# Token choice of the expert mixture on eight partition groups an expert, the prompt's residual rows stored after the first gather, and more unread transposes

## What is computed

```python
aff = jax.nn.softmax((xt @ router_w).astype(F32), axis=-1)
gates, idx = lax.top_k(aff.T, cap)          # cap = 2 * n_tok // 16
xe = xt[idx]
hid = jax.nn.silu(einsum(xe, w_gate)) * einsum(xe, w_up)
ye = einsum(hid, w_down) * gates[..., None]
y = zeros.at[idx.reshape(-1)].add(ye.reshape(-1, D))
```

## Time and profile before

| | |
|---|---|
| median of three runs | 2438.5 us |
| slowest and fastest run | 2439.77 and 2438.33 us |
| span of the profiled execution | 2439.0 us (within the range of the runs) |
| PE busy | 2353.6 us, 96% |
| DVE busy | 1783.9 us, 73% |
| ACT busy | 1362.2 us, 56% |
| POOL busy | 299.5 us, 12% |
| DMA | 577.38 MB, mean 237 GB/s |

### The profile page before, as it was taken

How to read it: one execution, slowest core, us unless ns; L and a number is a source line. 1 busy time by engine, 2 the same in 40 slices (tenths; PEclk the granted TensorE clock), 3 DMA queues, 4 the chain that set the end, 5 groups by cost and what they waited for, 6 DMA issues and landing times.

```text
span 2439.0 us, 34267 instructions
## 1 busy us (share of the span) xinstructions
PE 2353.6 (96%) x12062; PEld 1959.1 (80%) x12062; DVE 1783.9 (73%) x2053; ACT 1362.2 (56%) x1494; POOL 299.5 (12%) x360
## 2 busy tenths in 40 slices
PE   8999999999989999999999999998789999999997
PEld 7888888888768888888878888877578888888876
DVE  7565566465878888888865677765578888888854
ACT  5233233233457777777763555443257777777762
POOL 1000000000111112211111100000111211121011
PEclk9999999999989999999999999998899999999999
DMA  6424333223599999999970534231599999999931
GB/s 236 133 80 137 108 109 126 72 90 103 194 374 395 395 390 389 396 391 393 349 193 17 144 100 112 83 99 61 202 339 388 396 394 390 390 391 394 347 125 43
DMA packets 210973, 577.38 MB, mean 237 GB/s; under 512 B 24384, under 2 KB 65856, under 8 KB 210752
## 3 DMA queue, kind: packets, MB, share of 16 engines
q1 hardware_dynamic: 193584, 526.35, 57.7%
q0 software_dynamic: 17296, 49.83, 8.0%
HBM read 547.80 MB, written 30.43 MB: 237 GB/s over the span
## 4 chain that ended last, share of the span: by engine, by line
PE 90%; DVE 4%; DMA 3%; issue 1%; ACT 1%; POOL 0%; SPq 0%; DVEq 0%; POOLq 0%; ACTq 0%
PE bank L1575 43%; PE bank L1459 40%; PE bank L1396 4%; PE bank L1761 1%; PE bank L1743 1%; DMA rows_normed<-xn_late 1%; DVE d_parts L619 1%; DMA m_x<-rows_normed,idx_t 0%; DMA rows_summed<-m_y,idx_out 0%; DMA resid<-in_x_sample 0%; DMA raw<-in_ret_w_in 0%; ACT d_parts L610 0%; DVE top_i L1988 0%; DMA resid<-rows_summed 0%; DVE m_at L1990 0%
## 5 line engine op out<-in xcount | busy, mean ns | idle before, releaser
L2128 DVE TENSOR_TENSOR w_parts<-wt,w_parts 128x2048 fp32r<-128x2048 f32 x384 | 874.6, 2290 | 135.9 <-ACT w_parts L1157 126.1
L1157 ACT CAST w_parts<-wt 128x2048 fp32r<-128x2048 f32 x384 | 734.3, 1913 | 197.2 <-PE bank L1575 186.3
L1575 PE MATMUL bank<-w_parts,m_xt 128*128 128x512 f32 x2976 | 689.5, 391 | 2.1 <-ACT m_y L1215 2.1
L1575 PEld LDWEIGHTS bank<-w_parts,m_xt 128*128 128x128 f32 x2976 | 556.2, 188 | 117.6 <-issue 2.9
L1459 PE MATMUL bank<-d_parts,xt 128*128 128x512 f32 (+1 forms) x1872 | 383.4, 361 | 4.5 <-DVE d_parts L619 4.4
L1575 PE MATMUL bank<-w_parts,m_hidt 128*128 128x512 f32 x1632 | 384.0, 395 | 2.8 <-DVE m_hidt L2120 2.8
L1459 PEld LDWEIGHTS bank<-d_parts,xt 128*128 128x128 f32 x1872 | 315.9, 190 | 58.4 <-DVE d_parts L619 5.8
L1575 PEld LDWEIGHTS bank<-w_parts,m_hidt 128*128 128x128 f32 x1632 | 306.8, 190 | 66.7 <-issue 3.3
L619 DVE TENSOR_TENSOR d_parts<-raw,d_parts 128x512 fp32r<-128x512 f32 (+1 forms) x168 | 215.6, 1296 | 108.9 <-ACT d_parts L610 108.0
L610 ACT CAST d_parts<-raw 128x512 fp32r<-128x512 f32 (+1 forms) x168 | 183.4, 1107 | 198.9 <-PE bank L1459 195.1
L1459 PE MATMUL bank<-xt,d_parts 128*128 128x256 f32 (+1 forms) x1536 | 284.1, 340 | 5.2 <-DVE d_parts L619 1.9
(11 more groups left out here) (193 smaller groups left out, 2150.4 us busy)
## 6 DMA issues: line engine op xcount, KB each, us to landing
wt<-in_exp_w_gate SPq DMA_DIRECT2D x128, 1024.0 KB, 13.3
wt<-in_exp_w_up SPq DMA_DIRECT2D x128, 1024.0 KB, 12.5
wt<-in_exp_w_down SPq DMA_DIRECT2D x128, 1024.0 KB, 12.7
raw<-in_ret_w_in SPq DMA_DIRECT2D x32, 1024.0 KB, 5.2
raw<-in_na_w_in SPq DMA_DIRECT2D x24, 1024.0 KB, 5.3
raw<-in_ret_w_in SPq DMA_DIRECT2D x32, 512.0 KB, 4.6
raw<-in_ret_w_out SPq DMA_DIRECT2D x16, 1024.0 KB, 5.1
raw<-in_ple_w_gate SPq DMA_DIRECT2D x8, 1024.0 KB, 8.8
```

What stands on the lines that cost most here:

```text
L1157: nc.scalar.copy(w_parts[c % RING][:, 0, :], wt[:, place // 2, place % 2 * 2048:place % 2 * 2048 + 2048])\
L1575: last = nc.tensor.matmul(b[:, :], lhs[x][:, 2 * k + j, :], w[:, part, j, f * HALF:(f + 1) * HALF], start=(k == j == 0 and x == part == 0) ...
L2128: v.tensor_tensor(w_parts[c % RING][:, 1, :], wt[:, k // 2, k % 2 * 2048:k % 2 * 2048 + 2048], w_parts[c % RING][:, 0, :].bitcast(F32), AL ...
```

## The change

The choice is laid out on 128 partitions for the sample and 64 for the prompt: one copy of an expert's affinities for every round of eight. In every round all copies take their maximum and strike it out, except those copies whose own round has come: for these the values to be struck out are replaced by 4.0 (a mask, `held_back`), which matches nothing. After the last round one MAX8 and one index search serve all rounds. The results are spread by a mask (`of_round`), and small matmuls with a third mask (`of_expert`) bring them to `gate_t` and `idx_t`. The masks come in one small transfer on SP. The prompt's logits are ordered so that the 16 matmuls on the high parts need only ACT's copies. One activation of ACT ahead of the prompt's norm in layer 0 loads the table for exponents early. The prompt's residual is stored by SP between the landing of gather(0) and piece 10, and POOL (ahead of gather(1)), ACT (ahead of the first silu) and DVE (ahead of the first hidden product) wait for it. `m_x` and `m_hid` change places. `keep_busy` runs longer: 36 to 54 and 18 to 40 at the start, 20 to 34 ahead of layer 0's choice, 14 new ahead of the prompt's `affinities`, 36 to 46 ahead of `gate_t`, 36 to 54 ahead of the first rows, and twice 16 new at the end of layer 1's mixer.

```diff
-        m_x = put("m_x", [CAP, D], 144)
+        m_x = put("m_x", [CAP, D], 152)
-        m_hid = put("m_hid", [CAP, D], 152)
+        m_hid = put("m_hid", [CAP, D], 144)
...
+        def store_resid(eng, l, g):
+            first, n = GROUPS[g]
+            a, z = GROUP_TILES[g][0], GROUP_TILES[g][-1] + 1
+            eng.wait_ge(norm_sq[1 + 3 * l], nth(1 + 3 * l, z - 1))
+            if l:
+                for t in GROUP_TILES[g]:
+                    eng.dma_start(by_tile(rows_summed[l], l, g)[t - a], resid[:, t, :]).then_inc(resid_saved[l][g], 16)
+            else:
+                eng.dma_start(rows_summed[l][first:first + n, :].rearrange("(t p) d -> p t d", p=P),
+                              resid[:, a:z, :]).then_inc(resid_saved[l][g], 16)
...
                     if c == 10:
                         sp.wait_ge(moe_rows[l], 16)
+                        store_resid(sp, l, 0)
                     load(c, 0)
...
                 load_gain(3 * l + 2)
                 load_gain(3 * l + 3)
+                resid_stored(pool, l, 0)
                 matmuls_done(pool, f"rows{l}", "x1")
                 gather(1)
...
+                    if phase == "first":
+                        resid_stored(act, l, 0)
                     for f in range(2):
                         silu(f)
...
+            act.wait_ge(norm_rs[0], 1)
+            nc.scalar.activation(den[:, 0, 0:1], minus_half[:, 0:1], ACT.Exp)
...
+                if g == 0:
+                    b, full = fill(pe, route_phase(l, g), ("lg", g))
+                    for wk, xk in ((0, 0), (1, 0), (0, 1)):
+                        if wk == xk == 0:
+                            pe.wait_ge(norm_hi[m], 2 * nth(m, 1))
+                        elif xk:
+                            columns_ready(m, GROUP_TILES[g])
+                        for j in range(DT):
+                            last = nc.tensor.matmul(b[0:EXPERTS, 0:n], rw_parts[wk][:, l, j, :], xt[xk][:, j, first:first + n],
+                                                    start=(wk == xk == j == 0), stop=(xk == 1 and j == DT - 1))
...
-            keep_busy("ret", ("n0", 0, 0), 36)
+            keep_busy("ret", ("n0", 0, 0), 54)
-            keep_busy("ret", ("qk", 0, 0), 18)
+            keep_busy("ret", ("qk", 0, 0), 40)
...
+                keep_busy(f"route{l}", "idx", 14)
                 affinities(l, 0)
-                keep_busy(f"route{l}", "gate", 36)
-                pe.wait_ge(moe_top[l], 1)
-                for key, src in (("gate", top_v), ("idx", top_f)):
-                    b, full = fill(pe, f"route{l}", key)
-                    nc.tensor.transpose(b[0:CAP, 0:EXPERTS], src[:, :], ident[0:EXPERTS, 0:EXPERTS]).then_inc(full, 1)
+                keep_busy(f"route{l}", "gate", 46)
+                pe.wait_ge(masks_in, 16)
+                banks = [fill(pe, f"route{l}", key) for key in ("gate", "idx")]
+                for g in (1, 0):
+                    for k, (b, full) in enumerate(banks):
+                        pe.wait_ge(moe_picked[l], 2 * (1 - g) + k + 1)
+                        last = nc.tensor.matmul(b[(CAP_S, 0)[g]:(CAP, CAP_S)[g], 0:EXPERTS], picked[k][g][:, :],
+                                                of_expert[0:COPIES[g], :], start=True, stop=True)
...
-                keep_busy(f"rows{l}", "x0", 36)
+                keep_busy(f"rows{l}", "x0", 54)
...
-            keep_busy("route0", ("n1", 0, 0), 20)
+            keep_busy("route0", ("n1", 0, 0), 34)
...
+                    if k in ("norm0", "norm1"):
+                        keep_busy("naout", ("n4", int(k[4]), 0), 16)
...
-                v.tensor_tensor(x, x, wide(srec), ALU.mult).then_inc(moe_aff[l], 1)
+                nt, n = x.shape[1], ROUNDS[g]
+                each = x.rearrange("p t (a e) -> p t a e", a=1).broadcast_to([P, nt, n, EXPERTS])
+                factor = srec.rearrange("p (t a b) -> p t a b", a=1, b=1).broadcast_to([P, nt, n, EXPERTS])
+                v.tensor_tensor(m_rep[g][:, :, :].rearrange("p t (a e) -> p t a e", e=EXPERTS), each, factor, ALU.mult).then_inc(moe_aff[l], 1)
...
-                chain.link(v.max(out=top_v[:, c:c + 8], in_=a))
-                chain.link(v.max_index(out=top_i[:, c:c + 8], in_max=top_v[:, c:c + 8], in_values=a))
-                if k * 8 + 8 < n:
-                    chain.link(v.match_replace(out=a, in_to_replace=top_v[:, c:c + 8], in_values=a, imm_value=-1.0))
+                a, n = m_at[l][g][:, :], COPIES[g]
+                chain.link(v.max(out=top_v[0:n, :], in_=a))
+                if k < ROUNDS[g] - 1:
+                    chain.link(v.tensor_scalar(top_r[0:n, :], top_v[0:n, :], held_back[0:n, k:k + 1], None, ALU.max))
+                    chain.link(v.match_replace(out=a, in_to_replace=top_r[0:n, :], in_values=a, imm_value=-1.0))
+
+            def picked_rows(l, g):
+                a, n = m_at[l][g][:, :], COPIES[g]
+                chain.link(v.max_index(out=top_i[0:n, :], in_max=top_v[0:n, :], in_values=a))
+                pick(l, g, 0, top_v)
+                chain.link(v.tensor_copy(top_f[0:n, :], top_i[0:n, :]))
+                if g:
+                    chain.link(v.tensor_scalar(top_f[0:n, :], top_f[0:n, :], float(SEQ_P), None, ALU.add))
+                pick(l, g, 1, top_f)
```

More of the change, by code:

```diff
@@ L61 @@
 LAST_DOWN = {8: 2, 9: 3, 10: 4, 11: 7}
+TOP = 8
+ROUNDS = (CAP_P // TOP, CAP_S // TOP)
+COPIES = [EXPERTS * n for n in ROUNDS]
 NA_KEYS = [(0, 2, 0), (0, 2, 256), (2, 2, 512), (2, 3, 768), (3, 3, 768), (4, 2, 1152)]
@@ L369, in build @@
         mvr = sb("mvr", [P, TT])
-        top_v = sb("top_v", [EXPERTS, CAP])
-        top_i = sb("top_i", [EXPERTS, CAP], U32)
-        top_f = sb("top_f", [EXPERTS, CAP])
+        masks = sb("masks", [P, 2 * TOP + EXPERTS])
+        of_round, held_back, of_expert = masks[:, 0:TOP], masks[:, TOP:2 * TOP], masks[:, 2 * TOP:2 * TOP + EXPERTS]
+        top_v = sb("top_v", [P, TOP])
+        top_r = sb("top_r", [P, TOP])
+        top_i = sb("top_i", [P, TOP], U32)
+        top_f = sb("top_f", [P, TOP])
+        picked = [[sb(f"picked_{k}{g}", [COPIES[g], (CAP_P, CAP_S)[g]]) for g in range(2)] for k in "gr"]
         gate_t = sb("gate_t", [CAP, EXPERTS])
@@ L492, in build @@
         decay_in, first_gain_in = sem("decay_in"), sem("first_gain_in")
+        masks_in = sem("masks_in")
+        moe_picked = [sem(f"moe_picked{l}") for l in range(2)]
         const_in, bias_table, gn_in, ident_set = sem("const_in"), sem("bias_table"), sem("gn_in"), sem("ident_set")
@@ L520, in build @@
         moe_y_free = [sem(f"moe_y_free{l}") for l in range(2)]
-        resid_saved = [sem(f"resid_saved{l}") for l in range(2)]
+        resid_saved = [[sem(f"resid_saved{l}{g}") for g in range(2)] for l in range(2)]
         resid_in = [sem(f"resid_in{t}") for t in range(TT)]
@@ L1052, in logit_rows @@
                 b, done = filled(act, route_phase(l, g), ("lg", g))
-                nc.scalar.copy(m_at[l][g][:, :], b[0:EXPERTS, 0:GROUPS[g][1]]).then_inc(done, 1)
+                nc.scalar.copy(m_at[l][g][0:EXPERTS, :], b[0:EXPERTS, 0:GROUPS[g][1]]).then_inc(done, 1)
             def exponents(l, g):
@@ L1438, in affinities @@
                 b, full = fill(pe, route_phase(l, g), ("aff", g))
+                n = ROUNDS[g]
                 for k, t in enumerate(GROUP_TILES[g]):
-                    last = nc.tensor.transpose(b[0:EXPERTS, k * P:(k + 1) * P], m_lg[l][:, t, :], ident[:, :])
+                    last = nc.tensor.transpose(b[0:n * EXPERTS, k * P:(k + 1) * P], m_rep[g][:, k, :], ident[:, :])
                 last.then_inc(full, 1)
@@ L1978, in by_expert @@
                 else:
[L1979 removed]
+                    last = v.tensor_copy(m_at[l][g][:, :], b[0:COPIES[g], 0:n])
                 last.then_inc(done, 1)
```

75 lines of the change are left out of this document (42 added, 33 removed).

## The result

The changed kernel takes 2445.95 us (median of 9 runs, 2443.37 to 2447.93); the kernel before took 2438.5 beside it (9 runs, 2438.28 to 2443.47). The medians are 7.45 us apart; the ratio is 1.0024, 95% interval 1.0015 to 1.0032, which makes about 5.9 us: slower by 0.24%, clear of noise. Timed again later on another chip it took 2444.30 against 2438.98, ratio 1.0024 (1.0015 to 1.0034). The forecast was 2437.8 with a range of 2430 to 2443. The profiled execution took 2447.93 us with a span of 2446.2, 7.2 above the span of before. Of all executions behind this document one, of the run that stores the residual right behind the normed rows, took 7138 us and is not in its ratio.

The account below looks back on a forecast made before the run. PE, busy 96% of the span, bounds the kernel, so gains lie in its waits and slow stretches. Layer 0 -4.0 and layer 1 +3.3 (-5.2 + 6.8 + 1.7) give -0.7: median 2438.5 becomes 2437.8 us, range 2430 to 2443.

Parts of the forecast that it names:

- The choice of layer 0: Layer 0's token choice, DVE as the chain: index searches removed, small operations added, a wait gone; sum -3.6 us.
- C: Rival: the choice gets no shorter because operations on 128 partitions take longer; 2444.2 us, half of it 2441; chance 0.06.
- D: Rival: added transposes at 1.2 GHz, 0.23 us each, stand in the way; about +9 to +12, 2449 us; chance 0.02.
- the 4.0 us that layer 0 was to bring: Layer 0's total: -3.6 us from the choice and -0.4 up to the up product, together -4.0.
- not 2.75: Layer 1's choice: five rounds behind the last residual add shortened, less spreads and a wider product; about -2.75 us.
- the wait of gather(0) for the normed rows: Layer 1: with 1 MB of residual no longer ahead, 2.4 of the 2.8 us of waiting goes.
- the landing of the moved store: After gather(0): layer 0 store lands at 6.4 us, layer 1 at 14.0 (bounds 9.0 to 20.8), delaying gather(1).
- 0.4 of gain: Layer 0, gather(0)'s landing to the up product: gather(1) at 15.3, up product starts at 15.3 for 15.7, -0.4 us.
- B: Rival: store as slow as under loads, 10.8 and 20.8 us; 2450.8 us; decides above 26 us summed landings; chance 0.08.
- Rival A: Layer 1's two stores go side by side, landing at 9.0 us, no slow start; total -7.4, 2431.1 us; chance 0.22.
- of weight pieces none is late then: Layer 1: weight pieces queued on SP behind the moved store delay nothing, since PE itself comes later.
- Zero for the clock: Added transposes, including those at the start, cost zero each; 1 us of harm if some run at 1.2 GHz.

Follow-up runs that it names:

- the mended order: Changed kernel with layer 1's residual as four 256 KB transfers, 32 columns outermost, on SP, and POOL's wait for it behind gather(1): 2432.62 us, ratio 0.9972.

## Why the prediction was wrong

**Right.** The choice of layer 0: `idx_t` is done 3.6 us earlier once the 1.4 of the start are taken off (685.78 for 687.99), by the terms as they stood; 688 ns for the 128x512 maximum shows that 128 partitions cost no more (C is out). The new wait: in layer 1, by gather(1), held back by the residual store, with a slow up product of 12.94 behind it. D is out as well: the transposes ran at 0.11 us each (54 in 6.12).

**Right by luck.** In layer 1 `idx_t` came at 1770.60 (forecast 1770.2) and gather(0)'s rows at 1777.80 (forecast 1777.8). But these forecast times leave out the 4.0 us that layer 0 was to bring, and the changed kernel stood only 0.4 us ahead there (1726.45 for 1726.87). Counted from there, the choice gave 2.0 us and not 2.75; the wait of gather(0) for the normed rows went whole, 2.8 us and not 2.4, as the rows now follow `idx_t` by 7.2 us, no more than in layer 0 before. Together 4.8 for 5.2. Of what is missing of the choice, 0.4 are the 46 transposes ahead of `gate_t`, put at nothing with 5.3 us: in layer 1 they took 6.72, ended behind DVE's last spread, and the chain of waits goes through them.

**The step that failed.** The wait was foreseen, its size was not: the term that was mis-sized is the landing of the moved store. Layer 1: forecast 14.0 us after gather(0), measured 15.4; gather(1) 24.3 instead of 22.9, and the second turning over, itself slow after the wait, ran 0.6 us longer, which the sum left out. The up product started 8.8 us later against gather(0), not 6.8. Layer 0: forecast 6.4, measured 7.8 (693.44 to 701.2); gather(1)'s rows at 16.4 instead of 15.3. PE had 0.33 us of wait and a gate product of 13.68 us for 12.89, where 0.4 of gain stood. That gain could not have come from the landing: before, gather(1) landed at 10.6 and PE came at 15.7, so rows at 15.3 leave the up product where it was. Together about 3 us of the 7.9 by which the two profiled spans miss the forecast. The two landings sum to 23.2 (7.8 + 15.4), under the 26 from which B decides. Rival A had them side by side at 9.0; on SP's queue they were not that fast, and on POOL's, where its manner would hold, the later one needed 20.35.

**The step whose reason was wrong, though its number was near,** is the choice's -3.6 in layer 0, forecast as DVE's time alone. The run with the old store order shows that this gain reaches PE only if 1 MB ahead of gather(0) is gone: 10.6 us of gather without the move, 6.6 to 7.6 with it. The same holds in layer 1, where the forecast did say so. With the old order the choice is worth nothing, with the mended order 3.4 us, or 4.9 with the added transposes. The move thus gave more than the forecast credited to it, and the wait took it back.

**The sentence "of weight pieces none is late then"** held only under cover of the wait. In the changed kernel, too, the pieces of expert 1's gate weights issued from 1783 on take 20.6 us (median; 16.4 before); they stood at the front as soon as the wait was gone.

**Zero for the clock** is the other step that failed. 1.4 us at the start and 1.6 at the end of the profiled span are slow stretches of PE. Over fourteen profiles v1 took 7.3 to 8.6 us (7.3 to 7.9 in the five with the old transposes at the start) and the 18 matmuls 4.35 to 5.98, and no edit sorted them. They make 2.9 of the 5.0 us by which the first profile of the changed kernel is above the later one; layer 0's gate product (13.68 for 12.72) makes 1.0 more.

A third place goes with the choice. Ahead of the mixer's last product of layer 1 PE waits 2.12 us for the wider product of eight copies, 1.65 before; the forecast had that. It had nothing for the product itself. The product took 5.7 us in both profiles with the old choice and in three with the new one, the first of the changed kernel among them, but 7.3 in the other nine (granted clock 0.77 over 1735.5 to 1742.8 in the later profile of the changed kernel, 1.00 over 1740.5 to 1746 in the first). There 1.6 of the 2.0 us that the choice gave layer 1 are lost again. But the granted clock over 1650 to 1700 was 0.90 to 0.93 in those nine and only 0.76 to 0.87 in the other five, so a slow stretch seems to fall on one place or the other. Whether the wider product has a part in it is not shown.

Whether the changed kernel has more slow stretches on average stays open. Of the 7.9 us between the forecast and the two profiles the rows of the table from layer 0 to the loop make 4.7 less 0.4, the start and the end 3.6, and no run isolates the latter.

By the Trainium skill (DMA: Bandwidth & Descriptors, "Why a DMA increments its semaphore by 16 and not by 1") a transfer is cut into as many shares as divide its slowest dimensions, on SP's queue always on the lowest-numbered engines, on POOL's in turn. The times agree: four rows as outer dimension gave 15.4 us on SP, 32 columns 8.4, and on POOL the rate of two such stores rose from 0.05 to 0.108 MB/us. Which engines carried them no run here shows.

## What to carry to other kernels

Put a wait for a store at the first instruction that truly needs it, not ahead of a gather that PE is coming for; here one line moved and one access pattern turned made 12 to 13 us of difference. Before crediting a shorter chain to the engine that computes it, ask what the transfer behind it still has ahead of it in the DMA. And when a wait is found, ask what it covers: the next late thing was queued behind the same store. A forecast time that comes true proves its terms only if both are counted from the same point.

## What was not expected of the hardware

The same 1 MB of residual, stored beside weight loads, was complete after 8.4 us with 32 columns as outer dimension, after 15.4 with 4 rows on SP's queue, and after 21.5 with 4 rows on POOL's (1798.64 - 1777.16). A narrow store also delays the wide transfers behind it on its queue: the first 1 MB gate piece took 20.71 us behind it and 11.6 behind the spread form. And gather(0) of layer 0, with the same 96 rows, took 6.1 to 10.6 us by what was still ahead of it.
